# Two transformer blocks in float32 on one core: the norms' row factor behind the products, borders of stages overlapped, the value product in one item, the input loaded in parts

## The reference, cut to what matters

```python
for l in range(2):                                    # first_block
    x = x + 0.5 * swiglu(rmsnorm(x, ffn1_norm[l]), ffn1_w_gu[l], ffn1_w_down[l])
    x = x + hybrid_mixing(rmsnorm(x, mix_norm[l]), w_in[l], ...)   # MLA + pooling + FOX attention, @ w_out
    x = x + 0.5 * swiglu(rmsnorm(x, ffn2_norm[l]), ffn2_w_gu[l], ffn2_w_down[l])
x = rmsnorm(x, final_norm)
h = x                                                 # second_block, one layer
u = rmsnorm_2(h, norm_mix); p = u @ w_in_2            # windowed attention, RWKV-7, state space model
h = h + (merged @ w_out_2)
h = h + swiglu_2(rmsnorm_2(h, norm_ffn), ffn_w_gate_up_2, ffn_w_down_2)
return rmsnorm_2(h, norm_final)

def rmsnorm(x, g):  return x * rsqrt(mean(x * x, axis=-1) + eps) * g
def swiglu(h, w_gu, w_down):                          # hidden width 2816
    g, u = h @ w_gu[:, :2816], h @ w_gu[:, 2816:]
    return (silu(g) * u) @ w_down
```

## Time and profile before

| what | us |
|---|---|
| median of three runs (lowest, highest) | 3279.25 (3278.21, 3282.47) |
| profiled execution, span | 3278.0 |
| PE busy in it (share) | 3097.5 (94%) |
| DVE busy | 1331.2 (41%) |
| ACT busy | 1098.6 (34%) |
| POOL busy | 108.0 (3%) |
| PE's share of the chain that ended last | 88% |

### The profile page before, as it was taken

The page is one execution under the profiler, slowest core; times in us unless marked ns, Lnnn a source line. Parts: engine busy times, 40 slices in busy tenths (PEclk is TensorE's granted clock), DMA queues, the critical chain, the costliest instruction groups (busy, mean ns, idle before and its releaser), DMA issues.

```text
span 3278.0 us, 35599 instructions
## 1 busy us (share of the span) xinstructions
PE 3097.5 (94%) x13534; PEld 2288.9 (70%) x13534; DVE 1331.2 (41%) x1873; ACT 1098.6 (34%) x1570; POOL 108.0 (3%) x130
## 2 busy tenths in 40 slices
PE   7999999999998999999989999889799999989997
PEld 5888775678886888866468888435488344678886
DVE  3333455443335333354643333444444753243334
ACT  3333433433334333332633333231322101233333
POOL 0000011000000000001000000000000430000000
PEclk9999999999999999999999999999599999999999
DMA  3222220022222222221012222211000121222221
GB/s 120 96 96 96 81 88 26 26 82 97 98 101 78 88 99 98 87 86 70 1 58 93 96 96 100 93 58 58 20 1 2 39 77 58 96 92 96 96 93 71
DMA packets 44712, 246.50 MB, mean 75 GB/s; under 512 B 5352, under 2 KB 5544, under 8 KB 20800
## 3 DMA queue, kind: packets, MB, share of 16 engines
q1 hardware_dynamic: 43200, 238.62, 20.9%
q10 hardware_dynamic: 1008, 6.24, 0.5%
q0 software_dynamic: 400, 0.23, 0.0%
HBM read 243.06 MB, written 2.10 MB: 75 GB/s over the span
## 4 chain that ended last, share of the span: by engine, by line
PE 88%; DVE 7%; ACT 2%; issue 2%; DMA 1%; DVEq 0%; ACTq 0%; SPq 0%
PE psum L378 87%; DVE scr L1408 1%; PE psum L634 1%; DVE stat L1536 1%; DVE scr L1544 1%; DVE ring_lo L1427 0%; DMA g2s<-in_g2s 0%; DVE scr L1802 0%; DVE h_lo L1427 0%; DVE scr L1858 0%; DVE hid L1525 0%; DVE scr L1521 0%; DVE scr L1523 0%; DVE h L1411 0%; DMA cst<-in_cst 0%
## 5 line engine op out<-in xcount | busy, mean ns | idle before, releaser
L378 PE MATMUL psum<-highs 128*128 128x512 f32 (+2 forms) x3872 | 1364.1, 389 | 56.1 <-DVE h_lo L1427 47.1
L378 PE MATMUL psum<-highs,ring_lo 128*128 128x512 f32 x2456 | 963.6, 392 | 0.0
L378 PEld LDWEIGHTS psum<-highs 128*128 128x128 f32 x3872 | 730.1, 189 | 221.8 <-DVE h_lo L1427 43.7
L378 PE MATMUL psum<-h_lo,highs 128*128 128x512 f32 x1952 | 766.6, 393 | 0.0
L1427 DVE TENSOR_TENSOR ring_lo<-ring,highs 128x2048 fp32r<-128x2048 f32 (+1 forms) x158 | 353.8, 2240 | 999.3 <-ACT highs L1096 873.6
L378 PEld LDWEIGHTS psum<-highs,ring_lo 128*128 128x128 f32 x2456 | 465.0, 189 | 99.2 <-issue 0.6
L1096 ACT ACTIVATE highs<-ring 128x2048 fp32r<-128x2048 f32 x110 | 210.9, 1917 | 667.4 <-DMA ring<-in_wgu 632.0
L378 PEld LDWEIGHTS psum<-h_lo,highs 128*128 128x128 f32 x1952 | 370.4, 190 | 79.1 <-issue 1.2
L378 PE MATMUL psum<-h,ring 128*128 128x512 f32 x704 | 313.2, 601 | 9.2 <-DMA cst<-in_cst 8.3
L378 PEld LDWEIGHTS psum<-h,ring 128*128 128x128 f32 x704 | 135.4, 194 | 185.1 <-issue 175.6
L1427 DVE TENSOR_TENSOR highs<-hid,highs 128x512 fp32r<-128x512 f32 x220 | 152.3, 692 | 244.9 <-ACT highs L1112 151.2
(11 more groups left out here) (329 smaller groups left out, 2814.0 us busy)
## 6 DMA issues: line engine op xcount, KB each, us to landing
ring<-in_wgu SPq DMA_DIRECT2D x110, 1024.0 KB, 5.3
ring<-in_wmix SPq DMA_DIRECT2D x24, 1536.0 KB, 6.3
wdr<-in_wd SPq DMA_DIRECT2D x110, 256.0 KB, 2.6
ring<-in_wd SPq DMA_DIRECT2D x25, 1024.0 KB, 4.8
ring<-in_wmix SPq DMA_DIRECT2D x20, 1024.0 KB, 4.8
mixw<-in_wsmall ACTq DMA_DIRECT2D x3, 1280.0 KB, 5.5
ring<-in_wd SPq DMA_DIRECT2D x5, 512.0 KB, 3.8
x<-in_x SPq DMA_DIRECT2D x1, 2048.0 KB, 11.0
```

Source lines behind the costliest of these rows:

```text
L378: return nc.tensor.matmul(o, w, r, start=start, stop=stop, skip_group_check=True)
```

## The change

1. **Row factor behind the products.** `high` copies x times gain (a scale of the activation) into the high part without the row factor, `low_h` makes x*gain - high in one DVE operation, so the products of a stage start from x and the gain alone. The factor is computed beside them: ACT squares x into three buffers, POOL adds the eight blocks (`add_squares`, seven additions of [128, 512]), PE turns the sum into one column per 128 tokens (`row_sums`, four products with one column), ACT takes the root of [128, 4], DVE inverts it, PE spreads it over [128, 512] (`spread_r`, four products of 128 columns) and ACT copies it to `rms_r`. Every result is multiplied by it when it leaves PSUM: in each of the 22 passes of a feed-forward stage DVE multiplies gate and up half (two operations more), Silu then reads SBUF; in the mixer DVE takes latents, rope rows, gate rows, pooling input, queries and keys out with a factor (the queries and pooling input were ACT's), and values get it as ACT's scale. This holds for the seven split stages; the norm of the first block, the norm in front of the second block and the last norm stay as they were.
2. **Borders.** The first four blocks of x are updated, split and squared inside the second down phase; the last four and the next stage's first weight item, in two halves of 512 KB (`first_in`, `first_split`), behind it. The ring item with two row blocks comes first in the down phase instead of last, so that the slot of the next stage's first item comes free earlier. PSUM banks alternate (`b`, `o`). At the mixer's end and at the second block's end each block is updated, split and squared as its product ends.
3. **Values** in one item of 384 columns and 1.5 MB.
4. **Start.** x in four parts of 512 KB between the halves of the first weights; `gains` first, then 260 columns of `cst`; the rest of `cst` and `g2s` after the squares.
5. The outer loop over layers is written out; the first two and the last two passes of the feed-forward loop are taken out of it on ACT and DVE.

```diff
-            def gate_up(j, s, n0):
...
+            def row_sums(i, bank):
+                pe.wait_ge(sq_added, 7 * i + 7)
+                for t in range(NT):
+                    last = mm(psum[:, bank, t:t + 1], sumsq[:, t * P:(t + 1) * P], ones[:, 0:1], True, True)
+                last.then_inc(stat_mm, 1)
+            def spread_r(i, bank):
+                pe.wait_ge(rt_ready, i + 1)
+                for t in range(NT):
+                    last = mm(psum[:, bank, t * P:(t + 1) * P], rstd_tok[:, t:t + 1].to_broadcast([P, P]), ident, True, True)
+                last.then_inc(r_mm, 1)
...
+            def swiglu(f, n0, i, n, b):
+                o, par = 4 - b, n0 % 2
+                first_gate_up(n0, i, n, b)
+                row_sums(i, o + 3)
+                pe.wait_ge(ring_split, split_count(n0 + 1))
+                gate_up(0, 1, 1 - par, b, gate_ready)
+                spread_r(i, o + 2)
+                gate_up(1, 1, 1 - par, b, ring_free)
+                down1(0, 0, f, o, True, False)
...
-                for i, c0 in ((6, 0), (7, 256)):
+                w = item(6, 384)
+                for t in range(NT):
+                    c = slice(t * P, (t + 1) * P)
+                    for k in range(KD):
+                        last = mm3(psum[:, 1 + t, 0:384], (h_hi[:, k, c], h_lo[:, k, c]),
+                                   (w[0][:, k, :], w[1][:, k, :]), k == 0, k == KD - 1)
...
+            def high(k, n, gain):
+                act.wait_ge(x_upd, 8 * n + k + 1)
+                nc.scalar.activation(h_hi[:, k, :], x[:, k, :], ACT.Copy, scale=gain[:, k:k + 1]).then_inc(h_high, 1)
...
+            def low_h(k, i, gain):
+                dve.wait_ge(h_high, 8 * i + k + 1)
+                nc.vector.scalar_tensor_tensor(out=h_lo[:, k, :], in0=x[:, k, :], scalar=gain[:, k:k + 1],
+                                               in1=h_hi[:, k, :].bitcast(F32), op0=ALU.mult, op1=ALU.subtract)\
+                    .then_inc(h_split, 1)
...
+                    dve.wait_ge(gate_ready, f * NJ + j + 1)
+                    nc.vector.tensor_tensor(probs[:, s, :], psum[:, b + s, :], rms_r, ALU.mult).then_inc(gate_scaled, 1)
+                    dve.wait_ge(ring_free, used(n0 + j))
+                    nc.vector.tensor_tensor(up_r, psum[:, b + 2 + s, :], rms_r, ALU.mult).then_inc(up_scaled, 1)
...
+                for k in range(1, KD):
+                    pool.wait_ge(sq_ready, 8 * n + k + 1)
+                    if k > 1:
+                        pool.wait_ge(sq_added, 7 * i + k - 1)
+                    nc.gpsimd.tensor_tensor(sumsq, squares[0] if k == 1 else sumsq, squares[k % 3], ALU.add)\
+                        .then_inc(sq_added, 1)
```

More of the change, by code:

```diff
@@ L171, in build @@
         wd_hi = highs[:, 20:22, :]
[L173 to L176, removed]
+        foxv_hi = highs[:, 16:22, :].rearrange("p a b -> p (a b)")
+        out_hi = [hid_r[:, 4 * b:4 * b + 4, :].rearrange("p a b -> p (a b)") for b in range(2)]
+        z_lat = [hid[:, 2, :], hid[:, 0, :], hid[:, 1, :]]
+        z_sq = [hid[:, 3, :], hid[:, 4, :], hid[:, 5, :]]
+        sumsq, rms_r, up_r = tmp[:, 0, :], tmp[:, 1, :], tmp[:, 2, :]
+        squares = [tmp[:, 3 + b, :] for b in range(3)]
         y = d2[:, 0:8, :]
@@ L1221, in _ @@
-            norm(3 * LAYERS)
-            norm(3 * LAYERS + 1)
+                for m in range(KD):
+                    if m in (2, 4):
+                        split_out(m // 2 + 1)
+                    if m == 6:
+                        for half in range(2):
+                            split_first(nxt.n0, half, nxt.cols)
+                    high(m, nxt.n, nxt.gain)
+                    square(m, nxt.i)
+            for half in range(2):
+                for k in range(4 * half, 4 * half + 2):
+                    high(k, 0, STAGES[0].gain)
+                split_first(0, half, 2 * KD * P)
+                for k in range(4 * half + 2, 4 * half + 4):
+                    high(k, 0, STAGES[0].gain)
@@ new lines, in swiglu @@
+                    if k in EARLY_RESIDUAL:
+                        residual(*first_half[EARLY_RESIDUAL[k]])
+                    if nxt and k in EARLY_LOW:
+                        low_h(EARLY_LOW[k], nxt.i, nxt.gain)
+                if nxt:
+                    for half in range(2):
+                        low_first(nxt.n0, half, nxt.cols)
+                for m in range(4):
+                    if m < 3:
+                        residual(4 + m, b + m, down_ready, 6 * f + m + 4, scale)
+                    else:
+                        residual(7, b + 3, ring_free, used(n0 + FFN_ITEMS - 1), scale)
+                    if nxt and m:
+                        low_h(3 + m, nxt.i, nxt.gain)
@@ new lines, in _ @@
+            for l in range(LAYERS):
+                n0 = l * LAYER_ITEMS
+                swiglu(2 * l, n0, 3 * l, 4, STAGES[3 * l + 1])
+                mixer(l, n0 + FFN_ITEMS, 3 * l + 1, STAGES[3 * l + 2])
+                swiglu(2 * l + 1, n0 + FFN_ITEMS + MIX_ITEMS, 3 * l + 2, 0, STAGES[3 * l + 3] if l + 1 < LAYERS else None)
+            norm(3 * LAYERS, 0, gains[:, 0, G_FIN:G_FIN + 8], x)
+            dve.wait_ge(g2s_in, 16)
+            norm(3 * LAYERS + 1, 1, g2s[:, H_NM:H_NM + 8], h)
@@ L2002, in _ @@
                 pool.sem_inc(pooled, 1)
-                step.end()
+            for l in range(LAYERS):
+                add_squares(3 * l, 3 * l)
+                add_squares(3 * l + 1, 3 * l + 1)
+                mixer(l)
+                add_squares(3 * l + 2, 3 * l + 2)
             pool.wait_ge(gn_mm, 3)
```

683 lines of the change are left out of this document (410 added, 273 removed).

## The result

The changed kernel takes 3175.75 us (median of 4 runs, 3170.39 to 3178.07) against 3280.08 us for the kernel before, run on the same chip: ratio 0.969, 95% interval 0.967 to 0.970. Faster by 103 us by the ratio; 3176 were predicted. The profiled execution spans 3176.3 us.

What follows compares the result with a forecast made beforehand. PE was taken as the bound, busy 3097.5 of 3278.0 us. Gains and costs at borders, passes, start and mixers, 100.1 - 18.0 - 3.0 + 19.4 + 4.4 = 102.9 us, gave a forecast of 3176 us, range 3157 to 3203.

Steps and rivals of the forecast that it cites:

- Gaps of 86.8 and 12.9 of low clock removed: Six stage borders: PE's idle gaps between products, 86.8 us, and the low clock behind them, 12.9 us, would go.
- Row sums and spreading, 6 x 3.0: Six borders: short PE products cost 2.5 us (one-column 1.1, spreading 1.4), plus 0.5 for late sums; 18.0 us lost.
- Sums late at each stage: Rival, chance 0.20: POOL's additions or ACT's squares come late, PE waits 1 to 2 us, clock falls; 22 us worse, 3198.
- Start, 19.4: Kernel start: smaller first loads bring the first product at about 10 us and the second item's at 25.4; 19.4 us gained.
- First and last passes, 5 x 0.6: Five feed-forward stages: 0.3 us lost at the first pass and 0.3 at the last hidden block, 3.0 us together.
- Mixer, values 1.8 each: Value products in both mixers: one item of 384 columns, 20.4 us including idle time and low clock, against 22.2; 1.8 gained.
- Mixer, rest: Both mixers: PE's wait of 2.00 us for item 4's low part comes again, 0.4 us shorter in each.
- Loop, 0: Feed-forward loop: two added DVE operations of 0.7 us a pass cost nothing, covered by 3.6 us.
- DVE bounds the loop: Rival on the slower side, chance 0.03: chain over 3.6 us longer a pass; from 4.6, 110 us lost; at 5, 3330.
- Everything a little better: Rival, chance 0.08: values without idle time, one-column products at 0.11, start 3 us earlier; 19 us better, 3157.

Runs made afterwards that it cites:

- the run with five products: Changed kernel with five extra DVE products of 128 x 1536 values in each of 90 feed-forward loop passes: 3416.14 us, ratio 1.042.
- further edits: Changed kernel with additions of squares on DVE and two mixer edits: 3155.77 us; with the fourth block's work and additions also moved later in the down products: 3152.39 us.
- two products a pass: Changed kernel with two extra DVE products of 128 x 1536 values in each of 90 feed-forward loop passes: 3177.08 us, ratio 0.970.

## Why the prediction was right, and where it was not

The time was right, and so were the sign and the mechanism at the borders. That the sum came within 1.2 us is luck: the gain at the start was put too high, waits in the down products were left out, the borders' new cost was put too high and the mixers' gain too low, and these cancelled.

- **Borders.** *Gaps of 86.8 and 12.9 of low clock removed:* right. No PE wait at any of the six, clock 1.00. That it is the factor's place and the early blocks that do it was tested by putting each back: 63 us and 15 us. With the start's loads (7) and the values (7) that makes 92 of the 103; the rest wasn't assigned by a run.
- **Row sums and spreading, 6 x 3.0:** mis-sized. The two bounds for one column were 0.45 and 1.4 and I took 1.1, nearer to the full fp32 row; it is 0.92 behind three feed-forward stages and 0.81 behind the mixers and the second block. Spreading took 0.81, not 1.4: the row it was priced from has its records 0.17 us apart, these are 0.10 apart at the same clock of 1.00, so the nearest row was not near. 1.7 in all, and of the 0.5 a stage for late sums only 0.61 was spent, once, behind the second feed-forward stage (the expectation of one run calls it the second mixer). That is 1.3 a border less cost. But the sums were in time by 0.05 us at the first border, not by 1.4: the rival *Sums late at each stage* was that near.
- **Start, 19.4:** the step that failed. It gave 13.1: 46.7 - 31.1 for the second item's start, less 0.8 for spreading and 1.7 for the low clock behind the wait. The first product came at 11.2 (10 said) and the first 48 ended at 25.2 (23.5 said). Then "POOL's seven additions end at 23 to 25": they ended at 29.3. ACT's squares began at 16.1 instead of 14.3; each addition needs 1.29 and a hand-over, 1.44 instead of the 1.24 that came from four additions in a row; and the last was held for 2 us behind DVE's split. 4.18 us of wait, and 1.7 for the 24 products at the lower clock behind it. The prediction knew that a split can hold up the last addition: as a rival, 1 us late in each stage, with 0.5 in the sum. It happened at the borders too (1.9 us at the first), where the margin took it all but once. At the start, where all seven additions are on the path, there was no margin left and it came in full, on top of the late squares and the hand-overs.
- **Down products:** not in the prediction at all. It followed DVE's queue at the end of the stage, and not inside the down phase, where the new blocks were put: 1.86, 1.20 and 1.20 us. With POOL's additions cut they fell to 0.16 and nothing, so these additions cause them. The clock behind them stayed at 1.00.
- **First and last passes, 5 x 0.6:** the 0.3 for the last hidden block came in all five stages (0.33), the 0.3 at the first pass only once (0.18): 1.8 in place of 3.0.
- **Mixer, values 1.8 each:** too small. 3.7. The width gave 5.45 (5.6 said), the idle time was 1.73 (2.0 said), but the low clock I added behind it did not come. That too is luck: with the factor ahead, the second mixer waited 1.88 there, had a clock of 0.66 and took 18.45 us for these products instead of 16.9.
- **Mixer, rest:** the wait for the fifth item came (1.78, where 1.6 was said and 2.00 lay before). Of the 19.3 us of layer 0 another 2.9 belong to no edit: 1.3 in the attention, whose code is the same, and 1.6 in the output products, where the kernel before had the low clock behind its wait of 1.80 and in layer 1 did not. In layer 1 it is the low clock behind the fifth item's wait (0.66 in the kernel before) that did not come, 1.7 us. Against this, the stretch from the last value product to attention is 0.85 longer in both layers (26.96 against 26.1); seven of the 24 instances in the other runs have 26.2, so this is scatter as well.
- **Loop, 0:** right; its cover was mis-sized. The 3.6 us are those of the weights' chain (transfer, ACT, DVE), and I let DVE's other work push it one for one. But DVE waits 6.6 us for that chain in each pass, so added work fills this first. It begins to cost at 6.2 us more than the changed kernel has. The rival on the slower side had its threshold too near.
- **Rivals.** *Sums late at each stage* did not come, save at the start and, by 0.61, behind the second feed-forward stage. *DVE bounds the loop* is real as a mechanism, shown by the run with five products, 6 us away. *Everything a little better* (3157) did not come; further edits reach its time (3156 and 3152 us), but not by its own list.

What stays open: why attention takes 87.2, 89.4 or 90.8 us from one execution or layer to the next (below).

## What to carry to other kernels

A row factor can go behind a product, and then the norm's whole chain (sum, root, inversion) leaves the path; but its sum still has a due time. At a border it was met by 0.05 us; at the start, which has no stage ahead of it, it was missed by 4.2. Before giving a reduction to an engine because it is free, look at what its work holds up: POOL was free, but DVE's operations stood behind its additions, and DVE itself could make them in half the time (0.69 against 1.29 us) while it was idle. And the cover of a loop is found at the engine that gets the work, by adding up its own pass with its hand-overs, not from the chain that happens to be late next.

## What the runs showed of the hardware

**The granted clock after a short idle time isn't the same each time.** In the changed kernel PE waits 1.78 us for the fifth item in both mixers, ahead of the same products. Windows of 5 us behind each:

```profile
436.90:441.90 5.00, 5.00 (x15) 3.99 (x16) 2.58 (x4) 0.18 (x1) 4.69 (x5) 0.66 0.48 187
1417.60:1422.60 5.00, 4.98 (x22) 4.14 (x23) 2.62 (x4) 0.62 (x1) 4.69 (x5) 1.00 0.49 195
```

The clock is 0.66 of full speed in one and 1.00 in the other, 15 products against 22, 1.7 us. The kernel before has the same pair at its 1.80 us wait ahead of the output products: 0.66 from 621.9, 1.00 from 1650.8. Waits of 1.73 (ahead of the values) and 1.86 (down products) were followed by 1.00. The run with five products a pass has the largest sample, a wait in most passes of its loops, ahead of the same kind of products: of 63 waits of 1.79 to 1.92 us, 20 were followed by 0.66 over 5 us and 43 by 1.00. Behind longer ones it was mostly low, but not always equally: 0.50 from 29.4, behind 4.18; with the factor ahead, 0.50 behind 9.02, and behind three waits of 3.44 0.50 twice and 0.66 once; 0.72 behind 4.79. A wait of 3.05 in the second block was followed by 0.50 in the changed kernel and by 1.00 in two of the other runs (with the factor ahead, and with two products a pass). So what I charged for a wait of 2 us is what it can cost, not what it does.

**Attention with PE in short bursts shows the same.** Its two instances in the changed kernel have the same instructions:

```profile
505.95:593.20 87.25, 79.19 (x368) 42.04 (x369) 54.82 (x154) 53.58 (x155) 0.35 (x1) 1.00 0.00 1
...
1485.08:1575.92 90.84, 83.52 (x368) 44.78 (x369) 54.91 (x154) 53.69 (x155) 0.34 (x1) 0.94 0.00 1
```

87.25 us at clock 1.00, 90.84 at 0.94. Of the 26 instances in the changed kernel and the experiments 14 took 87.2 to 87.3 us, the others 88.6 to 90.9, in either layer. That alone is up to 7 us between two executions of one kernel, as much as the runs scatter (3170.4 to 3178.1), and the reason to read small edits from their own stage and not from the total.

**Products of one and of 128 columns in full fp32** stand 0.2 us apart here (0.92 and 0.81 us for four of either), and 384 columns in fp32r take 0.174.
